# Summing expert outputs with tokens on partitions in a one-core hybrid layer on Trainium2

## What is computed

```python
h = _rmsnorm(xp, norm2_g) * (1 + sc2) + sh2
xp = xp + g2 * _moe(h)                 # the same for the latent stream xs, with its own sc2, sh2, g2
y_prompt = _rmsnorm(xp, final_g)       # x * rsqrt(mean(x * x) + 1e-6) * final_g

# _moe: 32 experts, every token goes to its 4 best, weighted by a softmax over the 4 scores
hgu = xb @ w_gu[e] + b_gu[e]           # 1024 -> 2048
act = (h_lin + 1) * (h_glu * sigmoid(1.702 * h_glu))
ys = (act @ w_down[e] + b_down[e]) * gate
out[token] += ys
```

## Time and profile before

| | |
|---|---|
| median of three runs | 1348.68 us |
| the profiled execution's own time | 1353.32 us |
| its span, first to last instruction | 1351.6 us |
| mean granted TensorE clock | 0.929 of full speed |
| TensorE matmul busy, weight loads busy | 1146.9 us (85%), 583.1 us (43%) |
| VectorE busy, ScalarE busy | 280.2 us (21%), 263.3 us (19%) |
| chain that ended last, by engine | TensorE 49%, DMA 41%, VectorE 5% |
| loads of expert weights | 192 of 2 MB |

### The profile page before, as it was taken

One profiled execution on the slowest core, in us unless ns is written; L12 is line 12 of the kernel. 1 busy time (PEld: TensorE's weight loads), 2 busy tenths in 40 slices (PEclk: granted clock), 3 DMA queues, 4 the chain that ended last, 5 costly groups with the idle time before them and its releaser, 6 DMA issues.

```text
span 1351.6 us, 24840 instructions
## 1 busy us (share of the span) xinstructions
PE 1146.9 (85%) x10036; PEld 583.1 (43%) x10037; DVE 280.2 (21%) x850; ACT 263.3 (19%) x565; POOL 7.1 (1%) x27
## 2 busy tenths in 40 slices
PE   5999999999999977986897797876696688879885
PEld 2776887788873322332333232322232232323232
DVE  2179224421241100110111011010010011111013
ACT  2031226310031211221221121111121121111121
POOL 2000000000000000000000000000000000000000
PEclk7999999999987988998999899988898898989898
DMA  9988423244367899999999999999999999999994
GB/s 371 429 331 352 142 95 124 78 154 162 129 257 294 368 427 429 400 430 428 408 396 429 428 430 429 428 429 428 429 429 428 428 428 429 428 428 401 428 428 192
DMA packets 37307, 475.66 MB, mean 352 GB/s; under 512 B 5980, under 2 KB 7388, under 8 KB 8446
## 3 DMA queue, kind: packets, MB, share of 16 engines
q1 hardware_dynamic: 35296, 472.88, 83.9%
q10 hardware_dynamic: 1982, 2.36, 0.5%
HBM read 473.13 MB, written 2.10 MB: 352 GB/s over the span
## 4 chain that ended last, share of the span: by engine, by line
PE 49%; DMA 41%; DVE 5%; issue 2%; ACT 2%; DVEq 1%; SPq 0%
DMA big<-in_w_down 25%; DMA big<-in_w_gu 15%; PE bank L1078 14%; PE bank L1507 14%; PE bank L1539 6%; PE bank L1254 3%; PE bank L1468 2%; DMA big<-in_trunk_w 2%; DVE big L761 2%; PE bank L1432 2%; PE bank L1513 1%; ACT h L410 1%; PE bank L1066 1%; PE bank L1438 1%; DVEq L761 1%
## 5 line engine op out<-in xcount | busy, mean ns | idle before, releaser
L1507 PE MATMUL bank<-big,h 128*32 128x512 f32 x2816 | 378.1, 666 | 96.6 <-DMA big<-in_w_gu 93.3
L1507 PEld LDWEIGHTS bank<-big,h 128*32 128x32 f32 x2816 | 84.1, 116 | 328.9 <-issue 182.8
L1539 PE MATMUL bank<-big,h 128*32 128x256 f32 x2816 | 173.9, 396 | 59.4 <-DMA big<-in_w_down 51.0
L1078 PE MATMUL bank<-h,big 128*128 128x256 f32 x960 | 217.3, 385 | 1.5 <-DVE h L692 1.5
L1078 PEld LDWEIGHTS bank<-h,big 128*128 128x128 f32 x960 | 182.7, 193 | 31.2 <-issue 3.7
L410 ACT ACTIVATE side<-bank 128x256 f32<-128x256 f32 (+1 forms) x140 | 54.7, 392 | 613.2 <-PE bank L1432 395.1
L1539 PEld LDWEIGHTS bank<-big,h 128*32 128x32 f32 x2816 | 90.0, 114 | 131.4 <-DMA big<-in_w_down 54.3
L977 DVE TENSOR_SCALAR side<-iota,work 128x32 f32 (+1 forms) x90 | 17.4, 238 | 449.5 <-issue 449.5
L410 ACT ACT_TABLE_LOAD x68 | 87.2, 1283 | 6.0 <-PE bank L1290 1.7
L1037 DVE TENSOR_SCALAR h<-bank 128x256 f32<-128x256 f32 x44 | 18.7, 425 | 306.1 <-PE bank L1507 306.1
L410 ACT ACTIVATE big<-bank,par 128x256 f32<-128x256 f32 x60 | 26.8, 475 | 192.0 <-PE bank L1078 192.0
(11 more groups left out here) (233 smaller groups left out, 620.9 us busy)
## 6 DMA issues: line engine op xcount, KB each, us to landing
big<-in_w_gu SPq DMA_DIRECT2D x128, 2048.0 KB, 22.6
big<-in_w_down SPq DMA_DIRECT2D x64, 2048.0 KB, 27.7
big<-in_trunk_w SPq DMA_DIRECT2D x32, 2048.0 KB, 11.0
x<-in_x_t SPq DMA_DIRECT2D x1, 1024.0 KB, 4.9
out_y_t<-x ACTq DMA_DIRECT2D x4, 256.0 KB, 2.1
cinit<-in_c_init_t SPq DMA_DIRECT2D x1, 516.0 KB, 5.5
abias<-in_rpb SPq DMA_DIRECT2D x4, 128.0 KB, 22.3
out_c_new<-abias ACTq DMA_DIRECT2D x1, 512.0 KB
```

The lines of the kernel that those rows point to most:

```text
L1078: ins = pe.matmul(to, w[:, k, b * P:(b + 1) * P], src[:, k, :], start=k == 0, stop=k == KD - 1)
L1507: ins = pe.matmul(up_sum(q), mo["xg"][:, k % 2, k // 2, :], up_weights(expert_slot(e, j), i, q), start=False, stop=k == KD - 1, skip_group ...
L1539: ins = pe.matmul(bank[7][q * SLOTS:(q + 1) * SLOTS, 0:QW], mo["actt"][:, k % 2, k // 2, :], down_weights(expert_slot(e, GU_CHUNKS + j), i ...
```

## The change

The scatter changes its operands' places: the selection becomes the stationary operand and `y` the moving one, so tokens lie on partitions and channels along the free axis of banks 0 to 3 (`by_token`). The residual `x` is written into those banks ahead of the passes by 16 matmuls against the identity (`keep_residual`), in the place of the four `clear` matmuls: five ahead of the logits, four behind them, seven behind `up_bias`. There, 16 more matmuls spread the gate `g2` over four groups of 32 partitions; VectorE keeps it in SBUF. In a pass, VectorE multiplies bank 7 by `g2` for both streams into `y` (128 x 512) in the place of ScalarE's copy (128 x 256). The closing norm squares the banks on ScalarE with a sum along the free axis, multiplies by `final_g` (loaded as 128 copies of a row) on VectorE, and scales by one number for each token; VectorE scales the context stream and ScalarE the latent one, and SyncE issues the four stores, now of `y_tok`.

```diff
+        low = ctx.enter_context(nc.psum_tensor("low", [P, 4 * 512], F32))
+        bank = [low[:, 512 * i:512 * (i + 1)] for i in range(4)]
...
+        by_token = low[:, :].rearrange("p (q s c) -> p q s c", q=GROUPS, s=2)
...
@@ sync: at the end @@
+            for half in range(2):
+                for s in range(2):
+                    sp.wait_ge(S[f"y_ready{s}"], half + 1)
+                    cols = slice(half * D // 2, (half + 1) * D // 2)
+                    sp.dma_start(y_tok[:, s, cols], y_out[:, s, cols]).then_inc(S["y_stored"], 16)
...
@@ scalar: behind the load of bdn @@
+            act.wait_ge(S["wrs_ready"], 2)
+            act.wait_ge(S["shift_summed"], 1)
+            act.dma_start(final, bass.AP(final_g.tensor, 0, [[0, P], [1, D]])).then_inc(S["final_in"], 16)
...
@@ scalar: end of a pass @@
-                act.wait_ge(S["chunk_used"], n * PER_EXPERT + (N_TRUNK + PER_EXPERT))
-                keep(mo["y"], bank[7][:, 0:QW], "y_kept")
@@ scalar: behind the passes @@
-            for t in range(4):
-                act.wait_ge(S["mixed"], 4 + t + 1)
-                square(t)
-            norm_root(3)
-            for t in range(4):
-                act.wait_ge(S["y_ready"], 2 * t + 2)
-                act.dma_start(y_t[:, 2 * t:2 * t + 2, :], x[:, 2 * t:2 * t + 2, :]).then_inc(S["y_stored"], 16)
+            act.wait_ge(S["scattered"], 2 * GROUPS)
+            for pair in range(2):
+                if pair:
+                    act.wait_ge(S["gained"], 1)
+                for s in range(2):
+                    func(squares[:, pair, s], by_token[:, 2 * pair:2 * pair + 2, s, :], ACT.Square,
+                         accum_out=ss_pairs[:, pair, s:s + 1]).then_inc(S["ssq_tok"], 1)
+            act.wait_ge(S["var"], 3)
+            func(ss, ss, ACT.Sqrt).then_inc(S["root"], 1)
+            act.wait_ge(S["rstd_made"], 1)
+            for half in range(2):
+                part = y_out[:, 1, half * D // 2:(half + 1) * D // 2]
+                func(part, part, ACT.Copy, scale=ss[:, 1:2]).then_inc(S["y_ready1"], 1)
...
@@ vector: ahead of its wait for the table @@
+            dve.wait_ge(S["g2_made"], 1)
+            link(dve.tensor_copy(g2, bank[6][:, :].rearrange("p (s c) -> p s c", s=2)))
@@ vector: end of a pass @@
+                dve.wait_ge(S["chunk_used"], n * PER_EXPERT + (N_TRUNK + PER_EXPERT))
+                dve.tensor_tensor(mo["y"], bank[7][:, 0:QW].unsqueeze(1).to_broadcast([P, 2, QW]), g2, ALU.mult
+                                  ).then_inc(S["y_kept"], 1)
@@ vector: behind the passes @@
-            for t in range(4):
-                dve.wait_ge(S["scattered"], t + 1)
-                add_gated(40, t, 0)
-            dve.wait_ge(S["mixed"], 8)
-            dve.wait_ge(S["ssq"], 3)
-            rstd_from(bank[4][:, 0:TOK], D, RMS_EPS, "var", "root", 3)
-            for k in range(KD):
-                dve.scalar_tensor_tensor(x[:, k, :], x[:, k, :], pcol("final", k), rstd[:, :], ALU.mult, ALU.mult
-                                         ).then_inc(S["y_ready"], 1)
+            dve.wait_ge(S["final_in"], 16)
+            dve.wait_ge(S["scattered"], 2 * GROUPS)
+            for pair in (1, 0):
+                if pair == 0:
+                    dve.wait_ge(S["ssq_tok"], 2)
+                cols = slice(2 * pair * QW, 2 * (pair + 1) * QW)
+                for s in range(2):
+                    ins = dve.tensor_tensor(y_out[:, s, cols].rearrange("p (q c) -> p q c", q=2),
+                                            by_token[:, 2 * pair:2 * pair + 2, s, :],
+                                            final[:, cols].rearrange("p (q c) -> p q c", q=2), ALU.mult)
+                ins.then_inc(S["gained"], 1)
+            dve.wait_ge(S["ssq_tok"], 4)
+            link(dve.tensor_tensor(ss, ss_pairs[:, 0, :], ss_pairs[:, 1, :], ALU.add))
+            dve.tensor_scalar(ss, ss, 1.0 / D, RMS_EPS, ALU.mult, ALU.add).then_inc(S["var"], 1)
+            dve.wait_ge(S["root"], 3)
+            dve.reciprocal(ss, ss).then_inc(S["rstd_made"], 1)
...
+            for half in range(2):
+                part = y_out[:, 0, half * D // 2:(half + 1) * D // 2]
+                dve.tensor_scalar(part, part, ss[:, 0:1], None, ALU.mult).then_inc(S["y_ready0"], 1)
...
@@ tensor @@
-            for q in range(4):
-                clear(q)
+            def keep_residual(lo, hi):
+                for u in range(lo, hi):
+                    k, s = u // 2, u % 2
+                    pe.matmul(by_token[:, k // 2, s, (k % 2) * P:(k % 2 + 1) * P], x[:, k, s * L:(s + 1) * L],
+                              ident[:, :], start=u % 4 == 0, stop=False, skip_group_check=True)
+            keep_residual(0, 5)
             pe.wait_ge(S["lt_ready"], 1)
...
             ins.then_inc(S["logits_made"], 1)
+            keep_residual(5, 9)
...
-            def scatter(c):
+            def scatter(s):
...
-                    out.append(pe.matmul(bank[q][:, c * TOK:(c + 1) * TOK], mo["y"][rows_q, c * P:(c + 1) * P],
-                                         mo["selt"][rows_q, :], start=False, stop=False, skip_group_check=True))
+                    out.append(pe.matmul(by_token[:, q, s, :], mo["selt"][rows_q, s * L:(s + 1) * L],
+                                         mo["y"][rows_q, s, :], start=False, stop=False, skip_group_check=True))
...
             up_bias()
+            keep_residual(9, 16)
+            for s in range(2):
+                for c in range(2):
+                    for q in range(GROUPS):
+                        ins = pe.matmul(bank[6][q * SLOTS:(q + 1) * SLOTS, s * QW + c * P:s * QW + (c + 1) * P],
+                                        mod[:, 40 + 2 * q + c, s:s + 1].to_broadcast([P, SLOTS]), ident[:, :],
+                                        start=s + c == 0, stop=True, skip_group_check=True)
+            ins.then_inc(S["g2_made"], 1)
             pe.wait_ge(S["table_made"], 1)
             n_pass = table(pe, T_ALL, NE, MAX_PASS)
...
             pe.wait_ge(S["selt_kept"], n_pass + 1)
-            scatter(0)
-            for last in scatter(1):
-                last.then_inc(S["scattered"], 1)
-            norm_sum(3, bank[4][:, 0:TOK])
+            for s in range(2):
+                for last in scatter(s):
+                    last.then_inc(S["scattered"], 1)
```

More of the change, by code:

```diff
@@ L68 @@
 Z = {name: 4 * i for i, name in enumerate(PROJ)}
-PAR_WIDTHS = [("norm1", KD), ("norm2", KD), ("final", KD), ("b_mod", 48), ("b_in", 60),
+PAR_WIDTHS = [("norm1", KD), ("norm2", KD), ("b_mod", 48), ("b_in", 60),
               ("w_dw", 4 * CONV_W), ("b_dw", 4), ("cln_g", 4), ("cln_b", 4), ("mnorm", MH), ("cond", 2 * KD)]
@@ L87, in hybrid_layer @@
 def hybrid_layer(nc, trunk_w, w_gu, w_down, x_t, params, w_gate, b_gate, m_init, k_ctx_t, v_ctx,
-                 c_init_t, rpb, w_router, b_router, b_gu, b_down,
-                 y_t, k_new_t, v_new_t, c_new, n_new, m_new):
+                 c_init_t, rpb, w_router, b_router, b_gu, b_down, final_g,
+                 y_tok, k_new_t, v_new_t, c_new, n_new, m_new):
     with ExitStack() as ctx:
@@ L127, in hybrid_layer @@
         small = sb("small", [P, 192])
-        bank = [ctx.enter_context(nc.psum_tensor(f"bank{i}", [P, 512], F32)) for i in range(8)]
+        low = ctx.enter_context(nc.psum_tensor("low", [P, 4 * 512], F32))
+        bank = [low[:, 512 * i:512 * (i + 1)] for i in range(4)]
+        bank += [ctx.enter_context(nc.psum_tensor(f"bank{i}", [P, 512], F32)) for i in range(4, 8)]
+        by_token = low[:, :].rearrange("p (q s c) -> p q s c", q=GROUPS, s=2)
         def carve(base, at, shape, parts=P):
@@ L189, in hybrid_layer @@
         mo = carve_all(side, [("h_tok", [2, D]), ("gath", [QW]), ("selt", [TOK]), ("sel", [2, SLOTS]),
-                              ("selg", [2, GROUPS * SLOTS]), ("esel", [SLOTS], NE), ("y", [QW])])
+                              ("selg", [2, GROUPS * SLOTS]), ("esel", [SLOTS], NE), ("y", [2, QW])])
         mo |= carve_all(hf, [("xg", [2, GROUPS, SLOTS]), ("glu", [QW]), ("lin", [QW]), ("sig", [QW]),
                              ("act", [QW]), ("actt", [2, GROUPS, SLOTS])])
+        g2 = zf[:, (Z["om"] + 2) * TOK:(Z["om"] + 4) * TOK].rearrange("p (s c) -> p s c", s=2)
+        final = cinit[:, :, :, :].rearrange("p a b c -> p (a b c)")[:, 0:D]
+        xf = x[:, :, :].rearrange("p a b -> p (a b)")
+        y_out = xf.rearrange("p (s c) -> p s c", s=2)
+        squares = hf.rearrange("p (a s q c) -> p a s q c", a=2, s=2, q=2)
+        ss_pairs = sm["hsum"][:, 0:4].rearrange("p (a s) -> p a s", a=2)
+        ss = sm["hvar"][:, 0:2]
         bgu = mf[0:NE, :]
@@ L361, in _ @@
                     later_expert(turn * TURN + i, i)
+            for half in range(2):
[3 more added lines that the diff above has]
+                    sp.dma_start(y_tok[:, s, cols], y_out[:, s, cols]).then_inc(S["y_stored"], 16)
+            sp.wait_ge(S["y_stored"], 64)
         @block.gpsimd
@@ L1386, in _ @@
             ins.then_inc(S["raw_logits"], 1)
-            def clear(q):
```

(14 more changed lines are left out.)

5 lines of the change are left out of this document (3 added, 2 removed).

## The result

The changed kernel takes 1340.25 us, the median of twelve runs from 1336.24 to 1348.55; the kernel before, in twelve runs, takes 1348.95 (1342.31 to 1353.30). The ratio is 0.9944, with an interval of 0.9920 to 0.9968: 7.5 us less on a time of 1348.7, between 4.3 and 10.8 (the two medians alone lie 8.7 apart). So it is faster, where the forecast said 0.5 us less. Both profiled executions are the slowest of their twelve (1348.55 and 1353.30, spans 1346.8 and 1351.6), so the traces differ by 4.8 us only.

A forecast was written before the change was run, and what follows sets the result against it. Expert stage taken as a weight stream waiting on TensorE, so the start of pass 0 and the exposed tail count. +0.5, +6.0 and -7.0 make -0.5 on 1348.68: 1348.2 us, range 1341.0 to 1351.5.

The forecast's parts named there:

- that case's own range: Whole kernel: 1345.0 to 1351.0 us around the forecast, from the bounds of tail and insertion, not all at one end.
- the first rival: Full clock returns before pass 0: insertion half at full clock, pass 0 16.05 us, total -5.9, 1342.8 us; chance 0.21.
- pass 0: First expert pass: assumed to stay at 20.27 us, against 16.05 for pass 1, with the clock still low at its start.
- The sum: Whole kernel: +0.5 ahead of `up_bias`, +6.0 behind it, -7.0 in the tail, together -0.5 us.
- bare reading: TensorE's table readings ahead of pass 0 not covered by the spread: 1.2 us taken, between 0.9 and 2.9.
- The insertion: Seven blocks and the gate's spread behind `up_bias`: blocks 4.2, spread 2.0, reading 1.2, less 1.44, giving +6.0 us.
- In front of that: Routing around the logits: logits start 1.3 us earlier, four blocks behind them at half clock spend it again; +0.5 us.
- the rule cited there: TensorE's queue holds 64 instructions, so readings would begin with the spread, leaving 0.9 us bare, sum 0.3 lower.
- The tail: From the last down product to the end: 10.7 us in place of 17.75, -7.0 us, bounds -8.0 to -5.5.
- `y` on VectorE: In each pass: 0.69 us in place of ScalarE's 0.38, covered with 1.1 us to spare; no cost in 44 passes.
- the swapped scatter: In each pass: operands of the same sizes change places, eight matmuls either way; no cost.
- ScalarE's load of `final`: Row of `final_g`: load waits for `wrs_ready` within ScalarE's idle time; no cost, or one 1.3 us table load uncovered.

The follow-up runs named there:

- e1: Kernel before plus only the inserted blocks and spread behind `up_bias`, written to a bank nobody reads; 1350.51 us, ratio 1.0008.
- e3: Changed kernel with the gate's spread and VectorE's copy of it moved ahead of the output projection; seven blocks stay behind `up_bias`; 1337.70 us, ratio 0.9901.
- e4: Kernel before, its clears using a full block of zeros as weights in place of one row; 1346.46 us, ratio 0.9989.
- e8: As e3, but the count of passes read behind the passes and residual blocks dealt 8, 2, 6; 1336.72 us, ratio 0.9931.
- e2: Changed kernel with the spread early, eight blocks ahead of the logits, eight behind, nothing behind `up_bias`; 1334.16 us, ratio 0.9893.
- e11: Changed kernel with its residual blocks dealt 4, 8, 4 in place of 5, 4, 7; 1340.51 us, ratio 0.9915.
- e12: Changed kernel with VectorE's product for `y` made twice in every pass; 1340.86 us, ratio 0.9943.
- e7: As e2, but one of three table readings, the count of passes, moved behind the passes; 1331.02 us, ratio 0.9880.
- e6: Changed kernel run again without an edit; 1341.85 us, ratio 0.9955.
- e9: As e7, with eight blocks that nobody reads filling the pause behind `up_bias`; 1331.09 us, ratio 0.9846.
- e5: Kernel before run again without an edit; 1349.43 us in one run.
- e10: As e4, with eight blocks that nobody reads behind the logits; 1340.86 us, ratio 0.9949.

## Why the prediction was right or wrong

**The range held by a hair and the point missed.** The ratio on the forecast's base of 1348.68 gives 1341.1 us, 0.1 inside the range; the measured median, 1340.25, lies 8 us below the forecast of 1348.2, below 1341.0 and outside that case's own range. That the range held owes nothing to the forecast: it had been drawn wide enough to take in the rival. What happened is the first rival, "the clock comes back before pass 0" (1342.8, given 0.21).

**The step that failed: pass 0.** The sum took its 20.27 us as unchanged, for the reason that TensorE had worked for most of 395.30 to 410.50 us and the clock had stayed low. It took 16.22 and 16.23: -4.1, since the clock came back 1.9 and 2.3 us ahead of it and not 8.7 us into it, and held across the bare reading of 1.52 us. Where the clock was low through `up_bias`, it came back ahead of the pass in all four profiles with seven blocks behind it (the changed kernel's two, e1, e3), and in none of the four with six or none (the kernel before's two, e4, e8). In e1 the inserted work was all there was of the change, and a bare reading of 1.99 us lost the clock again. Whether it is the kind of work that counts (the routing has one-row weights, 32-column matmuls and transposes, the insertion full blocks) is not shown: in e4 the clock came back 3.0 us into the pass with nothing inserted, in e8 at the same point behind six blocks.

**The insertion was right in kind and too large**: +4.4 in place of +6.5. Behind `up_bias` it was 6.49 us less 1.44, +5.05 and not +6.0: the blocks took 3.36 us, 0.24 for each instruction and not 0.30 (two small matmuls, L1417, were a poor row for fourteen in a row), the spread 1.75 and not 2.0, as the clock rose within it, and the bare reading 1.52, not 1.2. In front of that it was -0.65 and not +0.5: the logits began 1.34 us earlier, counted from the sum of squares, as forecast, and they and the eight instructions behind them ran at full clock, ahead of the fall.

The bare reading also bears on the rule cited there. The prediction took 407.62 us for the time at which the table was made, from the bracket of ScalarE's row; that is when ScalarE fell idle. The table's own row in the kernel before is

```profile
407.43 0.23 DVE L1013 CAST tab<-work 1x163 int32<-1x163 f32 x1
```

so the table was made at 407.66, by luck nearly the same, and the three readings last some 2.85 us (2.89 in e2, with nothing queued beside them). From the start of the spread to the pass it is 3.28 us in the changed kernel and 3.16 to 3.19 in e1, e11 and e12, so the readings began near the spread's start, some 0.4 us behind it if they took as long. Behind 28 queued instructions (e3) they were covered whole. That agrees with the 64 places of TensorE's queue in the Trainium skill, "Advanced Engine Details and Errata", section "Engine Queue Depths"; the 0.9 us that I worked out by the rule were 1.52, as the readings began that much later and the spread was shorter.

**The tail was right.** With the last scatter at full clock, e2, e3, e7, e8 and e11 take 9.81 to 9.88 us from its start to the end, and the traced execution of the old kernel 16.82: -7.0, as forecast. With the scatter at half clock it is 10.74 to 10.82 (the changed kernel, e6, e9, e12) against 17.72 and 17.75 (e1, e4), again -7.0. In e5 and e10 the old sums over partitions ran faster as well, and against their 15.8 it is -6.0. From the end of the last down product, e2 takes 10.8 us (1321.61 to 1332.4; forecast 10.7) and the profiled run of the change 12.6, with half the clock in `up_bias` and the scatter. I found nothing that says which runs have the lower clock there.

**`y` on VectorE, the swapped scatter, ScalarE's load of `final`: nothing, right.** Passes at full clock take 16.05 before and 16.12 after, and e12 shows the slack.

**The account.** Forecast -0.5, less 4.1 for pass 0 and 2.1 for the insertion, is -6.7, or -5.7 with the tail at -6.0; measured -7.5, with an interval that holds both. No run shows the change without the clock's part.

**What stays open.** What brings the clock back, and why the same routing runs at 0.71 in one execution and 0.90 in another. It makes some 4 us (21.60 and 17.70), a third of the 12 us between the fastest and the slowest run of the change, whose mean clocks are 0.948 and 0.933. Also open is a part of e9's gain: its ratio is worth 20.8 us (the medians 18.3), of which 7.7 lie between the sum of squares and the end of pass 0 and 6.1 in the tail. The long stretch from pass 1 to the last scatter varies from 899.6 to 905.5 us over all traces, and the stretch ahead of the sum of squares from 381.0 to 388.3, neither with an order by kernel; together they hide the rest.

## What to carry to other kernels

Price work ahead of a TensorE-bound stage with the clock that it leaves behind: 4.4 us of matmuls that nobody needed put the start of the passes off by 4.9 us, and the stage behind them got back 2.5 (e1). When a first pass is slower than the second, look at where the clock falls and where it comes back, in short windows, and not at the mean of the pass alone: 17.55 us at 0.92 was a late return in one run (e8), 17.74 at 0.90 a fall behind a pause in another (e7). A pause of 2.5 us behind a fast stage cost 1.6 us of pass (e7 and e9), and work that must be done anyway is best placed where the pause is. Look at the clock in more than one execution before giving a difference of 4 us to an edit.

## What was unexpected of the hardware

TensorE's clock fell in the routing though the engine was hardly idle: in the kernel before it fell 0.25 us behind 3.69 us of one-row matmuls without a pause. With full blocks at the same place it fell 3.7 us later, counted from the sum of squares (e4, 0.9 us less to pass 0), and with eight more behind the logits it held at 1.00 through the stage (e10). That the one-row matmuls are the cause is not shown: the changed kernel has none, and its clock fell at about the same point. Reading one number more from the table costs TensorE's sequencer 0.65 us (e2 and e7), or nothing when enough full-size matmuls stand queued ahead of it (e3). And matmuls whose result nobody reads cost nothing that the times could tell behind `up_bias` in the old kernel (e1), and with such matmuls behind its logits and full-row clears it was faster (e10).
